# Two transformer blocks in fp32r on one core: in the up products, four matmuls with high weights and then four with low ones

## The reference, cut to what matters

```
u2 = rmsnorm(h, norm_ffn_g)
up = centred_dwconv3(u2 @ ffn_w_up) + ffn_conv_b      # 2048 -> 11264
h  = h + (silu(a) * gv) @ ffn_w_down                  # a, gv: the halves of up
...
h = einsum("cd,chkd->chk", x, peer_u[experts])        # as x @ peer_u.T, all experts
y = einsum("chk,chkd->cd", gelu(h) * gates, peer_v[experts])
```

## Time and profile before

| | |
|---|---|
| median of 3 runs | 3494.06 us (3490.4 to 3494.12) |
| the profiled execution | 3497.53 us, of which the profile's span is 3495.8 us |
| PE busy | 3328.6 us (95%), 21834 matmuls |
| DVE, ACT busy | 2185.1 us (63%), 1597.4 us (46%) |
| DMA | 590.60 MB, mean 169 GB/s |

### The profile page before, as it was taken

How to read it: one execution, slowest core, us unless ns; L and a number is a source line. 1 busy time by engine, 2 the same in 40 slices (tenths; PEclk the granted TensorE clock), 3 DMA queues, 4 the chain that set the end, 5 groups by cost and what they waited for, 6 DMA issues and landing times.

```text
span 3495.8 us, 54346 instructions
## 1 busy us (share of the span) xinstructions
PE 3328.6 (95%) x21834; PEld 2921.1 (84%) x21834; DVE 2185.1 (63%) x2954; ACT 1597.4 (46%) x2110; POOL 3.5 (0%) x10
## 2 busy tenths in 40 slices
PE   7999999999999998887988889999999999999999
PEld 6999998788888886786778879888888888888887
DVE  5664455666566566675359986676666566755554
ACT  4554434454455454456443334434444444434453
POOL 0000000000000000000000000000000000000000
PEclk9999999999999999998999999999999999999999
DMA  6445655555555555431243333544555555555554
GB/s 219 165 156 182 208 184 178 184 187 191 189 186 190 190 186 171 135 125 55 91 172 133 136 133 134 193 172 167 175 172 174 182 184 175 173 180 186 193 185 168
DMA packets 161113, 590.60 MB, mean 169 GB/s; under 512 B 17888, under 2 KB 17920, under 8 KB 159584
## 3 DMA queue, kind: packets, MB, share of 16 engines
q1 hardware_dynamic: 160624, 586.69, 49.2%
q0 software_dynamic: 240, 0.44, 0.1%
HBM read 584.96 MB, written 2.10 MB: 168 GB/s over the span
## 4 chain that ended last, share of the span: by engine, by line
PE 86%; DVE 10%; ACT 2%; issue 1%; DMA 1%; SPq 0%; DVEq 0%; ACTq 0%
PE PS L403 20%; PE PS L361 12%; PE PS L363 12%; PE PS L362 12%; PE PS L404 10%; PE PS L371 6%; PE PS L372 5%; PE PS L373 5%; DVE LO L287 3%; PE PS L1209 2%; PE PS L956 2%; DVE GB L927 1%; DVE TK L1043 1%; DVE TK L1046 1%; PE PS L622 0%
## 5 line engine op out<-in xcount | busy, mean ns | idle before, releaser
L287 DVE TENSOR_TENSOR LO<-RAW,HI 128x1024 fp32r<-128x1024 f32 (+1 forms) x1096 | 1330.3, 1219 | 922.3 <-ACT HI L286 915.6
L286 ACT ACTIVATE HI<-RAW 128x1024 fp32r<-128x1024 f32 (+1 forms) x1096 | 1149.4, 1054 | 1182.0 <-PE PS L363 620.8
L403 PE MATMUL PS<-XX,HI 128*128 128x512 f32 x2944 | 1045.2, 400 | 1.2 <-DVE LO L287 1.2
L404 PE MATMUL PS<-XX,LO 128*128 128x256 f32 x2944 | 826.6, 281 | 0.0
L403 PEld LDWEIGHTS PS<-XX,HI 128*128 128x128 f32 x2944 | 553.1, 188 | 137.1 <-ACT HI L286 1.5
L361 PE MATMUL PS<-HI,FH 128*128 128x512 f32 x1504 | 593.9, 395 | 20.2 <-DVE FL L499 16.6
L371 PE MATMUL PS<-XX,HI 128*128 128x256 f32 x1920 | 557.0, 290 | 47.3 <-DVE LO L287 29.1
L363 PE MATMUL PS<-HI,FL 128*128 128x512 f32 x1504 | 587.2, 390 | 0.0
L362 PE MATMUL PS<-LO,FH 128*128 128x512 f32 x1504 | 586.4, 390 | 0.0
L404 PEld LDWEIGHTS PS<-XX,LO 128*128 128x128 f32 x2944 | 556.2, 189 | 0.2
L372 PE MATMUL PS<-XX,HI 128*128 128x256 f32 x1920 | 548.3, 286 | 0.0
(11 more groups left out here) (234 smaller groups left out, 2359.8 us busy)
## 6 DMA issues: line engine op xcount, KB each, us to landing
RAW<-in_peer_v SPq DMA_DIRECT2D x256, 512.0 KB, 3.2
RAW<-in_peer_ut_rest SPq DMA_DIRECT2D x192, 512.0 KB, 3.3
RAW<-in_ffn_w_up SPq DMA_DIRECT2D x176, 512.0 KB, 4.2
RAW<-in_w_in SPq DMA_DIRECT2D x136, 512.0 KB, 4.1
RAW<-in_ffn_w_down SPq DMA_DIRECT2D x88, 512.0 KB, 3.8
RAW<-in_peer_ut SPq DMA_DIRECT2D x64, 512.0 KB, 3.2
RAW<-in_w_mix_out SPq DMA_DIRECT2D x32, 512.0 KB, 3.3
RAW<-in_w_in_2c SPq DMA_DIRECT2D x32, 512.0 KB, 3.3
```

The lines of the kernel that those rows point to most:

```text
L286: hi_done.append(AC.do(lambda e, raw=raw, hi=hi: e.activation(hi, raw, ACT.Copy), landed[i], used))
L287: lo_done.append(DV.do(lambda e, raw=raw, hi=hi, lo=lo: e.tensor_tensor(lo, raw, hi.bitcast(F32), ALU.subtract), hi_done[i], landed[i], used))
L403: e.matmul(o, hi[:, k, w], x, start=u == 0 and k == 0, stop=False, skip_group_check=True)
L404: m = e.matmul(o[:, 0:S], lo[:, k, w], x[:, 0:S], start=False, stop=u == 3 and k == 3, skip_group_check=True)
```

## The change

Inside `product_both`, for each c, the loop over k is cut in two: first the four wide matmuls, then the four narrow ones. The 16 matmuls of a unit, their weights, their streamed columns and their outputs stay the same, and so do the unit's waits and its mark; `XH[:, 4u + k, :]` is the same memory as the first 256 columns of `x`. The sums are added in another order.

```diff
@@ -399,9 +399,10 @@
                     o = bank(2 * pair + c)
                     w = slice(128 * c, 128 * c + 128)
                     for k in range(4):
-                        x = XX[:, 4 * u + k, :, :].rearrange("p h s -> p (h s)")
-                        e.matmul(o, hi[:, k, w], x, start=u == 0 and k == 0, stop=False, skip_group_check=True)
-                        m = e.matmul(o[:, 0:S], lo[:, k, w], x[:, 0:S], start=False, stop=u == 3 and k == 3,
+                        e.matmul(o, hi[:, k, w], XX[:, 4 * u + k, :, :].rearrange("p h s -> p (h s)"),
+                                 start=u == 0 and k == 0, stop=False, skip_group_check=True)
+                    for k in range(4):
+                        m = e.matmul(o[:, 0:S], lo[:, k, w], XH[:, 4 * u + k, :], start=False, stop=u == 3 and k == 3,
                                      skip_group_check=True)
                 return m
```

## The result

| | before | after |
|---|---|---|
| median of 20 runs | 3495.64 us (3490.4 to 3499.84) | 3488.59 us (3486.13 to 3490.88) |
| ratio, 95% interval | | 0.9979, 0.9972 to 0.9985 |
| profiled execution | 3497.53 us | 3488.52 us |

The change makes the kernel 7.05 us faster by the medians, 0.2%, where 14.6 us were forecast. By the interval of the ratio the gain is 5 to 10 us, so noise doesn't cover the difference. The time lies in the stated range of 3470 to 3489 us, but only by 0.4 us, and outside the forecast's own range of 3475 to 3484; the wide range was made to take in the rivals, so it is no merit of the sum. The kernel before also ran once at a mean granted clock of 0.84 in place of 0.98 and took 3727.07 us; that run is left out of every comparison here.

What follows compares the result with a forecast made beforehand. TensorE's own row of instructions was taken to bound the kernel; 736 blocks, each 3 x 6.6 = 19.8 ns shorter, give 14.6 us, so 3494.06 becomes 3479.5 us. Own range 3475 to 3484, with rivals 3470 to 3489.

Steps and rivals of the forecast that it cites:

- The bound, and what moves: Whole kernel: TensorE bounds it, busy 3328.6 of 3495.8 us; only the neighbours of 2944 wide and 2944 narrow matmuls change.
- the gain is given back: Rival, stretches with gates: DVE or transfers become the bound, at most 3.9 us lost, 3483 us; counted within the forecast's 0.80.
- Spacings of pure runs: Matmuls in runs of their own kind: wide after wide 226.7 ns each, narrow after narrow 120 ns each.
- That the extra goes with the change of width and not with the tile: Alternating pairs: the 6.6 ns beyond pure-run spacings comes from changing width, not from the tile streamed.
- every matmul keeps its price: Rival, up stretches: wide over XX costs 236 ns and narrow 117 in any order, time stays 3494 us; chance 0.10.
- One time down and up 6.6: Each block after the change: its one remaining change of width down and up costs 6.6 ns in all.
- A block after: Eight matmuls of one unit and one c, regrouped: 1393.4 ns, 19.8 ns less than before, over 736 blocks 14.6 us.
- wide after wide: Down stretch from 825.71 to 912.77 us: 384 wide matmuls at 226.7 ns each.
- The first wide one pays for the narrow run: Rival, each block's narrow-wide border: late weight load, 310 ns in place of 236, 40 us slower, 3534 us; chance 0.05.
- More than forecast: Rival, narrow runs: spacing 113 ns in place of 120, up to 40 us faster, 3454 us; chance 0.05.

Runs made afterwards that it cites:

- all-wide: Beside the kernel before, low weights too multiply both parts of the activations, so all 16 matmuls of a unit are wide; 3793.88 us.
- all-narrow: Beside the kernel before, each wide matmul is cut into two of 256 columns, making 24 narrow matmuls a unit; 3517.02 us.
- three in other banks: c made the inner loop, against the c-outer orders with runs of one, two and four matmuls; 3498.52, 3480.23 and 3488.27 us.
- snake: Against eight wide then eight narrow in every unit, odd units go narrow first; 3480.62 us against 3496.22 for the kernel before, ratio 0.9954.
- two and two: Against the changed kernel, two wide then two narrow matmuls, twice for each c; 3482.20 us, ratio 0.9959 to the kernel before.
- two-unit kernel: Against one unit at a time, 16 wide matmuls of two units, then their 16 narrow; both units' buffers freed together; 3540.81 us, ratio 1.0122.

## Why the prediction was half right

*The bound, and what moves.* Right. The stretches of these matmuls are as long as TensorE's own row, the idle time ahead of them stayed, and 368 units x 20 ns = 7.4 us account for the 7.05 measured. The rival in which the gain is given back had nothing to give back.

*Spacings of pure runs.* Right: 226.7 and 120 were confirmed by the all-wide and the all-narrow kernel, over the very tiles in question.

*That the extra goes with the change of width and not with the tile.* Right, by the same kernels and by the three in other banks. The rival "every matmul keeps its price" falls, though its time, 3494, was nearer to the measured 3488.59 than the forecast's 3479.5: by luck, since its prices are wrong and only their sum came close.

*"One time down and up 6.6" in "A block after".* This is the step that failed: the block was put at 1393.4 ns and took 1403. The 6.6 ns were measured where a change comes after every single matmul, and were carried over to runs of four as a fixed price. The price depends on the length of the run:

| run of wide and of narrow | ns a unit | changes a unit | extra a change, ns | wide ones lose | narrow ones save |
|---|---|---|---|---|---|
| 1 (before) | 2826 | 8 | (2826 - 2773.6) / 8 = 6.6 | 9.4 | 2.8 |
| 2 | 2786 | 4 | 3.2 | 13.1 | 9.6 |
| 4 (the change) | 2806 | 2 | 16 | 22.5 | 5.8 |
| 8 | 2793 | 1 | 19 | 27.4 | 7.5 |
| 16 (snake) | 2783 | 1/2 | 19 | 27.4 | 7.6 |

The last two columns are means over the single starts of a stretch, in ns a run, against 226.7 and 120 a matmul; their difference can be half a ns above the column before, which has the stretch's first matmuls in it. The price is thus made of two parts. Wide ones after a change are slow, by 5 to 6 ns on average, until, in runs of eight or more, the sixth. Narrow ones after a change are quicker than 120. In runs of two the wide ones lose 13 ns and the narrow ones save 10, so that the two nearly cancel; in runs of four they lose 22 and save only 6. Of all the lengths tried, four is the worst but one. The forecast gain of 19.8 ns a block came out as 10.

*What I could have seen.* The earlier trace rows show two spacings, 0.23 and 0.24, behind the last narrow matmul, and I read them as two instances of one price. They are one cost that lingers: the second of them has a wide one ahead, and by "wide after wide" it should have been 0.227. A few more starts would have given 825.71 to 826.87 for five wide ones, 232 each (and ten such at 1093.66). Instead I took the wide run's mean over 384, in which the five at the start add less than 0.1 ns.

*The first wide one pays for the narrow run.* It didn't, in any kernel: the first behind 4, 8 or 16 narrow ones takes 233 to 235, not 310. This rival had the right border but the wrong size. *More than forecast* wanted narrow ones at 113 throughout; in the changed kernel's runs of four they take 119 on average.

*What the page gives.* The Trainium skill, "TensorE: Matmul & The Clock Gate", section "Back-to-back issue gap", gives the isolated gap at the full clock as N / 2.4 + 2.5 ns for N columns, about 216 and 109 here, and about 131 ns for 512 columns in a stream of loads and matmuls. The rows agree with neither: they have 226.7 and 120 in pure runs, and between changes of width 224 to 241 and 112 to 120 by what stood before.

Not settled is what in TensorE makes wide matmuls slow for a while. The runs exclude the tile streamed, the bank, the weights' columns and the wait for data; they don't show a mechanism for it. A rival that no run tests is the weight loads, of which every matmul here has one: in the all-narrow kernel PEld is busy for 184.00 of the 184 us from 919, in the all-wide one for 191.34 of the 231 from 966, so the loads could have a part in the spacings. Nor does anything here say how a run of three, or of unlike lengths, would do.

## What to carry to other kernels

A spacing between two kinds of neighbours is no fixed price: read ten or more starts behind each change of kind before it is multiplied by a count, and measure the order wanted at more than one run length, because the cost of a change of width went up and down with it (3 ns a change at two, 16 at four, 19 at eight). Where units follow each other, alternate which kind comes first, which doubles the runs without holding a buffer longer; the snake has the shortest unit here and is 15.6 us below the one before, and two and two, a change of three lines, is within 2 us of it, which the runs' intervals can't tell apart. Grouping that frees several buffers at once can cost far more in waits than the order brings.

## What the runs showed of the hardware that was not expected

- Spacing of fp32r matmuls that each load new weights, at the full granted clock: 226.7 ns for 512 columns and 120.0 for 256 in pure runs. Twice 113.3 is 226.7, and 113 is also what the first 256-column one behind a settled wide run takes.
- Behind eight or more narrow ones, wide ones run at 233, 236, 228, 233 and 231 ns and then at 227. Where runs are too short to settle, single wide ones go at 224 to 241, on average 236 in runs of one, 233 in runs of two and 232 in runs of four, and behind the last narrow one it took five, nine or ten wide ones to settle.
- Busy sums of a line change by hundreds of us with the order alone (L403 and L404 before: 1045.2 + 826.6 us; L402 and L405 after: 805.8 + 468.3) while the time changes by 7.
- Where the two-unit kernel waited 2 to 4 us again and again, some of the wide matmuls behind a wait were 427 ns apart: the granted clock was at its lower level (1.2 GHz) there, as in the run at 991.23, ahead of which TensorE had idled for 2.53 us. Its mean over 931 to 1127 us was 0.98 where the kernel before has 1.00.
